# A hybrid decoder block on eight cores: SSM weight preparation on DVE, a fifth x buffer, u stores in POOL's queue, W_o casts later

## The reference, cut to what matters

```python
xn = rms_norm(x, g_pre_mix)
q, k, v, u = split(xn @ w_in)              # 1024, 256, 256, 1024 columns
attn = sliding_window_attention(rotary(q), rotary(k), v, sinks)   # window 128
y = s5_ssm(u)                              # 64 groups of 16 channels, 64 complex states each
z = gelu(y); ssm = z * sigmoid(z @ w_glu + b_glu)
mix = concat(rms_norm(attn), rms_norm(ssm)) @ w_o
h = x + rms_norm(mix)
out = h + rms_norm(swiglu(rms_norm(h)))    # gate, up: 2048 x 5632; down: 5632 x 2048
```

## Time and profile before

| | us |
|---|---|
| median of 3 runs (2626.15 to 2682.37) | 2632.01 |
| profiled execution, time | 2620.06 |
| profiled execution, span of the slowest core (core 3) | 2618.5 |
| span of the fastest core | 2595.2 |
| PE busy | 2445.9 (93%) |
| DVE, ACT, POOL busy | 1524.8, 848.9, 618.6 |

### The profile page before, as it was taken

One profiled execution on the slowest core, in us unless ns is written; L12 is line 12 of the kernel. 1 busy time (PEld: TensorE's weight loads), 2 busy tenths in 40 slices (PEclk: granted clock), 3 DMA queues, 4 the chain that ended last, 5 costly groups with the idle time before them and its releaser, 6 DMA issues.

```text
span 2618.5 us, 33812 instructions; the slowest of 8 cores (2595.2 to 2618.5 us)
## 1 busy us (share of the span) xinstructions
PE 2445.9 (93%) x12896; PEld 1203.6 (46%) x12896; DVE 1524.8 (58%) x2354; ACT 848.9 (32%) x1654; POOL 618.6 (24%) x708
## 2 busy tenths in 40 slices
PE   3797888987998989999999999999999999999998
PEld 2443656843444434444444444444444444444443
DVE  7735673668687687777777400016877877710003
ACT  7633443366565433223222100003222223200002
POOL 3334576854343200101010111100010101111112
PEclk9898888998999999999999999999999999999999
DMA  8499568466797977666766966649999876775557
GB/s 217 135 147 124 94 97 142 75 159 157 181 205 206 184 147 132 89 89 83 94 81 90 191 106 110 105 68 162 178 177 179 135 93 81 96 116 79 74 106 239
DMA packets 484893, 341.82 MB, mean 131 GB/s; under 512 B 182016, under 2 KB 448640, under 8 KB 475776
## 3 DMA queue, kind: packets, MB, share of 16 engines
q0 software_dynamic: 257744, 168.90, 47.4%
q1 hardware_dynamic: 226992, 170.77, 25.5%
HBM read 406.65 MB, written 63.96 MB: 180 GB/s over the span
## 4 chain that ended last, share of the span: by engine, by line
PE 81%; DMA 7%; DVE 6%; issue 2%; POOL 2%; ACT 1%; SPq 1%; POOLq 0%; DVEq 0%; ACTq 0%
PE ps L433 81%; DMA ws.6_48<-w_in 1%; DVE M1.2_44 L433 1%; DMA A1T.68_110<-A1.44_86 1%; SPq L433 1%; DMA raw.148_190<-w_up 1%; DMA PT.126_168<-Pb.123_165 1%; DMA uring.89_131<-uscr 0%; DVE ast.27_69 L433 0%; DMA A1T.66_108<-A1.44_86 0%; DVE hn.142_184 L433 0%; DMA raw.146_188<-w_gate 0%; DVE TT.49_91 L433 0%; DVE TT.50_92 L433 0%; DVE Rb.102_144 L433 0%
## 5 line engine op out<-in xcount | busy, mean ns | idle before, releaser
L433 DVE TENSOR_TENSOR hf.234_276<-ps,gpo.189_231 128x512 f32<-128x512 f32 x16 | 11.1, 691 | 243.4 <-ACT junk.144_186 L433 233.7
L433 ACT ACTIVATE junk.144_186<-ps 128x512 bf16<-128x512 f32 x48 | 28.6, 597 | 296.3 <-PE ps L433 291.1
L433 PE MATMUL ps<-hnT.143_185,wsm.151_193 128*128 128x512 bf16 x528 | 121.1, 379 | 0.4 <-DVE ev.171_213 L433 0.4
L433 PE MATMUL ps<-hnT.143_185,wsm.150_192 128*128 128x512 bf16 x528 | 121.3, 379 | 0.0
L433 PE MATMUL ps<-hnT.143_185,wsm.153_195 128*128 128x512 bf16 x528 | 121.1, 379 | 0.0
L433 PE MATMUL ps<-hnT.143_185,wsm.152_194 128*128 128x512 bf16 x528 | 121.1, 379 | 0.0
L433 ACT ACTIVATE ps<-ps 128x512 f32<-128x512 f32 x32 | 18.6, 582 | 294.8 <-DVE ev.175_217 L433 138.5
L433 DVE TENSOR_TENSOR wsm.153_195<-raw.149_191 128x1024 bf16<-128x1024 bf16 x110 | 68.6, 684 | 61.7 <-DMA raw.149_191<-w_gate 59.5
L433 POOL DMA_DIRECT2D raw.146_188<-w_gate x22 | 25.2, 1144 | 266.3 <-PE ps L433 182.8
L433 POOL DMA_DIRECT2D raw.148_190<-w_up x22 | 25.2, 1145 | 255.9 <-PE ps L433 117.4
L433 POOL DMA_DIRECT2D raw.149_191<-w_gate x22 | 25.1, 1141 | 251.6 <-PE ps L433 132.2
(11 more groups left out here) (1349 smaller groups left out, 6263.8 us busy)
## 6 DMA issues: line engine op xcount, KB each, us to landing
raw.146_188<-w_gate POOLq DMA_DIRECT2D x22, 1024.0 KB, 9.4
raw.147_189<-w_up POOLq DMA_DIRECT2D x22, 1024.0 KB, 9.4
raw.149_191<-w_gate POOLq DMA_DIRECT2D x22, 1024.0 KB, 11.2
raw.148_190<-w_up POOLq DMA_DIRECT2D x22, 1024.0 KB, 12.3
woscr<-w_o POOLq DMA_DIRECT2D x16, 512.0 KB, 8.4
xr.137_179<-x SPq DMA_DIRECT2D x8, 1024.0 KB, 7.2
xr.138_180<-x SPq DMA_DIRECT2D x8, 1024.0 KB, 6.3
hscr<-xr.137_179 SPq DMA_DIRECT2D x8, 1024.0 KB, 4.1
```

What stands on the lines that cost most here:

```text
L433: inst = getattr(eng, m)(*a, **kw)
```

## The change

1. x tiles have five buffers, the fifth in space that the GLU uses later, taken in the order `XBUF`. The buffers in `ws[1]` hold tiles 3, 4, 8 and 9 only. The first w_in load is cut by columns, and tiles from 4 on wait for the first part alone. Only the first halves of even tiles are copied by ACT, the others by DVE.
2. The rope tables wait for the scaling of the last x tile.
3. For blocks 0 to 2 `prep` makes `CL` on DVE; blocks 1 and 2 wait for the scaling of tile 13.
4. u is stored through POOL's queue, each block as soon as its last group is copied; the second half of u runs over token blocks inside column blocks.
5. The sums of k and q are made on DVE.
6. Six W_o casts wait for pairs 14 to 29, ten for copies of the rope; the casts of w_glu wait for pairs 16 to 25.
7. Smaller ones: the last token block of `M1` is scaled at priority 590; the output projection scales before it squares, and squares into PSUM; attention tiles are spread over one tile more; the load of unit 2 waits for tile 14.

```diff
-        xt = [sb("xt", o_, [128, 2048], F32) for o_ in (SO, SO + 8 * KB, WSO + 16 * KB, WSO + 24 * KB)]
+        xt = [sb("xt", o_, [128, 2048], F32) for o_ in (SO, SO + 8 * KB, c1 + 2944, WSO + 16 * KB, WSO + 24 * KB)]
+        XBUF = (0, 1, 2, 3, 4, 0, 1, 2, 3, 4, 0, 1, 2, 0, 1, 2)
...
-        load_w(0, 1536, wk=("wu",))
+        for i in range(2):
+            P.dma(ws[0][:, :, 256 * i:256 * i + 256], w_in_v[:, :, 1536 + 256 * i:1792 + 256 * i], q="gpsimd", wk=[("wu", i)])
...
-                P.dma(b[:, :], x[tt * 128:(tt + 1) * 128, :], rk=[("wu", 0), ("wu", 1)] if tt > 3 else ())
+                P.dma(b[:, :], x[tt * 128:(tt + 1) * 128, :], rk=[("wu", 0)] if tt > 3 else ())
...
-                if h == 0 or tt % 2 == 0:
+                if h == 0 and tt % 2 == 0:
                     A.activation(out=dst, in_=src, func=AF.Copy)
...
-        V.tensor_copy(out=posf[:, :], in_=posi[:, :])
+        P._dep(V.tensor_copy(out=posf[:, :], in_=posi[:, :]), xsop[15], True)
...
+            if b in (1, 2):
+                P._dep(first, xsop[13], True)
+            E = V if b < 3 else G
...
-            G.tensor_tensor(out=o(c, 9), in0=bc(Cf, 0, 9), in1=lk(0, 8, 9), op=ALU.mult)
+            E.tensor_tensor(out=o(c, 9), in0=bc(Cf, 0, 9), in1=lk(0, 8, 9), op=ALU.mult)
...
-            for tb in range(4):
-                for blk in range(4):
+            for n in range(16):
+                tb, blk = (n // 4, n % 4) if h == 0 else (n % 4, n // 4)
...
+                if n >= 12 if h == 0 else n % 4 == 3:
+                    c0 = (4 * h + blk) * 128
+                    P.dma(uscr[:, c0:c0 + 128, :].rearrange("j p c -> p j c"), ust[:, 3 - blk, :, :], q="gpsimd", wk=[("u", 4 * h + blk)])
...
-                G.tensor_tensor(out=qb, in0=rA[:, :], in1=rB[:, :], op=ALU.add)
+                V.tensor_tensor(out=qb, in0=rA[:, :], in1=rB[:, :], op=ALU.add)
...
-                E_ = G if i0 < 4 else V
+                E_ = V
...
+                if tb == 3:
+                    P.prio = 590.0
...
-                A.activation(out=junk[cb % 2][:, :], in_=ps[:, cb % 2, :], func=AF.Square, scale=1.0 / math.sqrt(D),
+                V.tensor_tensor(out=Ab[:, cs], in0=ps[:, cb % 2, :], in1=gpm[:, cs], op=ALU.mult)
+                A.activation(out=ps[:, cb % 2, :], in_=ps[:, cb % 2, :], func=AF.Square, scale=1.0 / math.sqrt(D),
                              accum_out=ss[:, cb:cb + 1])
-                V.tensor_tensor(out=Ab[:, cs], in0=ps[:, cb % 2, :], in1=gpm[:, cs], op=ALU.mult)
...
-                  rk=[("hn", 15)] if blk == 0 and u == 2 else (), lat=12.0 if blk == 0 and u < 2 else 0.0)
+                  rk=[("hn", 14)] if blk == 0 and u == 2 else (), lat=12.0 if blk == 0 and u < 2 else 0.0)
...
-            if q % 4 == 1:
-                cast_wo(4 + q // 8, q // 4 % 2, P.ops[-1])
-            if q % 4 == 3:
-                P.prio = 20.0
-                cast_wo(q // 8, q // 4 % 2, usteps[16 + q // 2])
+            if q in (14, 17, 20, 23, 26, 29):
+                cast_wo((14, 17, 20, 23, 26, 29).index(q), last)
-            if q % 8 == 4:
-                i = q // 8
-                P.dma(glscr[:, i, :], w_glu_v[:, 4 + i, :], q="gpsimd", after=(P.ops[-1],), wk=[("gl", i)])
+            if q in (16, 19, 22, 25):
+                i = (16, 19, 22, 25).index(q)
+                P.dma(glscr[:, i, :], w_glu_v[:, 4 + i, :], q="gpsimd", after=(last,), wk=[("gl", i)])
...
+        for n, i in enumerate((10, 18, 22, 26, 30, 34, 38, 42, 46, 50)):
+            P.prio = 62.0
+            cast_wo(6 + n, psteps[i])
...
-            for at in range(min(NT, LOOK + (NT - LOOK) * tt // (NT - 3)), min(NT, LOOK + (NT - LOOK) * (tt + 1) // (NT - 3))):
+            for at in range(min(NT, LOOK + (NT - LOOK) * tt // (NT - 2)), min(NT, LOOK + (NT - LOOK) * (tt + 1) // (NT - 2))):
```

More of the change, by code:

```diff
@@ L604, in frac @@
             V.tensor_tensor(out=dst, in0=src, in1=tmp, op=ALU.subtract)
+        xsop = []
         def xnorm(tt):
-            b, s = xt[tt % 4], xs[tt % 2]
+            b, s = xt[XBUF[tt]], xs[tt % 2]
             if tt > 0:
-                P.dma(b[:, :], x[tt * 128:(tt + 1) * 128, :], rk=[("wu", 0), ("wu", 1)] if tt > 3 else ())
+                P.dma(b[:, :], x[tt * 128:(tt + 1) * 128, :], rk=[("wu", 0)] if tt > 3 else ())
             ms, r = col(), col()
@@ L613, in xnorm @@
             rstd(r, ms)
-            V.scalar_tensor_tensor(out=s[:, :], in0=b[:, :], scalar=r, in1=gbc[:, :], op0=ALU.mult, op1=ALU.mult)
+            xsop.append(V.scalar_tensor_tensor(out=s[:, :], in0=b[:, :], scalar=r, in1=gbc[:, :], op0=ALU.mult, op1=ALU.mult))
             for h in range(2):
@@ L737, in prep @@
             CL, A1, A1T, kt = CLs[b % 3], A1s[b % 2], A1Ts[b % 3], KTs[b % 3]
-            V.tensor_tensor(out=o(a, 8), in0=bc(Bb, 0, 8), in1=lk(0, 0, 8), op=ALU.mult)
+            first = V.tensor_tensor(out=o(a, 8), in0=bc(Bb, 0, 8), in1=lk(0, 0, 8), op=ALU.mult)
+            if b in (1, 2):
+                P._dep(first, xsop[13], True)
+            E = V if b < 3 else G
             V.tensor_tensor(out=o(b_, 8), in0=bc(Bb, 1, 8), in1=lk(1, 0, 8), op=ALU.mult)
@@ L744, in prep @@
             P.dma(A1T[:, :, :], A1[:, :], transpose=True)
-            G.tensor_tensor(out=o(c, 9), in0=bc(Cf, 0, 9), in1=lk(0, 8, 9), op=ALU.mult)
[L746 to L750, removed]
+            E.tensor_tensor(out=o(c, 9), in0=bc(Cf, 0, 9), in1=lk(0, 8, 9), op=ALU.mult)
+            E.tensor_tensor(out=o(d, 9), in0=bc(Cf, 1, 9), in1=lk(1, 8, 9), op=ALU.mult)
+            E.tensor_tensor(out=oC(0), in0=o(c, 9), in1=o(d, 9), op=ALU.add)
+            E.tensor_tensor(out=o(c, 9), in0=bc(Cf, 1, 9), in1=lk(0, 8, 9), op=ALU.mult)
+            E.tensor_tensor(out=o(d, 9), in0=bc(Cf, 0, 9), in1=lk(1, 8, 9), op=ALU.mult)
+            E.tensor_tensor(out=oC(1), in0=o(c, 9), in1=o(d, 9), op=ALU.subtract)
             for par in range(2):
@@ L771, in bank3 @@
             return bk
-        usteps = []
         def proj_u(h):
             sl = ws[h % 2]
-            for tb in range(4):
-                for blk in range(4):
+            for n in range(16):
+                tb, blk = (n // 4, n % 4) if h == 0 else (n % 4, n // 4)
+                if True:
                     bk = bank3()
@@ L783, in proj_u @@
                                      rhs=xnT[:, c, tb * 512:(tb + 1) * 512], start=(c == 0), stop=(c == 15))
[L784 to L788, removed]
+                    A.activation(out=ust[:, 3 - blk, :, tb * 64:(tb + 1) * 64],
+                                 in_=ps[:, bk, :].rearrange("p (c j) -> p j c", j=8), func=AF.Copy)
+                if n >= 12 if h == 0 else n % 4 == 3:
+                    c0 = (4 * h + blk) * 128
+                    P.dma(uscr[:, c0:c0 + 128, :].rearrange("j p c -> p j c"), ust[:, 3 - blk, :, :], q="gpsimd", wk=[("u", 4 * h + blk)])
         RK = WSO + 16 * KB
@@ L809, in load_h @@
             return w
+        psteps = []
         def rope(bk, tt, n):
             rr, rA, rB = rbuf[n % 2]
-            A.activation(out=rr[:, :], in_=ps[:, bk, 0:256], func=AF.Copy)
+            psteps.append(A.activation(out=rr[:, :], in_=ps[:, bk, 0:256], func=AF.Copy))
             V.tensor_tensor(out=rA[:, :], in0=rr[:, :], in1=cap(cosT, tt * 32, [[512, 128], [0, 8], [1, 32]]), op=ALU.mult)
@@ L1046, in build_nc, with cast_wo @@
         woscr = dscr("woscr", [8, 128, 2, 2048], BF16)
-        def cast_wo(k, i, op):
-            P.dma(woscr[k, :, i, :], w_o_v[:, 2 * k + i, :], q="gpsimd", after=(op,), wk=[("wo", k, i)])
+        def cast_wo(n, op):
+            P.dma(woscr[n // 2, :, n % 2, :], w_o_v[:, n, :], q="gpsimd", after=(op,), wk=[("wo", n // 2, n % 2)])
         def load_wo(k):
@@ L1287, in build_nc @@
             P.prio = 60.0 + q
-            if q % 4 == 1:
-                cast_wo(4 + q // 8, q // 4 % 2, P.ops[-1])
-            if q % 4 == 3:
-                P.prio = 20.0
-                cast_wo(q // 8, q // 4 % 2, usteps[16 + q // 2])
-            if q % 8 == 4:
-                i = q // 8
-                P.dma(glscr[:, i, :], w_glu_v[:, 4 + i, :], q="gpsimd", after=(P.ops[-1],), wk=[("gl", i)])
+            last = P.ops[-1]
+            if q in (14, 17, 20, 23, 26, 29):
[3 more added lines that the diff above has]
+                P.dma(glscr[:, i, :], w_glu_v[:, 4 + i, :], q="gpsimd", after=(last,), wk=[("gl", i)])
             if q % 4 == 3 and q < 20:
```

## The result

The changed kernel took 2659.71 us (median of 6, 2652.69 to 2747.14) against 2629.08 for the kernel before (6 runs beside it, 2623.73 to 2682.37): a ratio of 1.0109, 95% interval 1.0076 to 1.0142. So it is about 1% slower, inside the 2% that the prediction took for no change. The forecast was 2570, with a range of 2538 to 2612.

What follows compares the result with a forecast made beforehand. The prediction took TensorE's idle and low-clock time before 957 us as the bound; terms -33 + 2 - 22 + 3 - 6 - 6 = -62 gave 2558 for the profiled execution and 2570 for the median, range 2538 to 2612.

Steps and rivals of the forecast that it cites:

- Front, -33 to 114: 0 to 147 us: earlier x tiles and cheaper prep end the first half of u at 114, saving 33 (19 to 41).
- Transposes, -22: Stall at 225 to 267: moving W_o casts away ends late A1 transposes, saving 22 (8 to 28).
- u stores, +2: Before the first u tile: eight u stores in POOL's queue land later, costing 2 (0 to 10).
- the hold-up of +5.5: u stores: if DVE copies of 0.69 held up each of eight POOL stores, their cost would be +5.5, not +2.
- K and q, +3 (-10 to +22): 300 to 545 us: ten casts arrive and 48 sums move from POOL to DVE, costing 3 net.
- The rival with casts at 4.4: K and q stretch: ten moved casts cost 4.4 each, 44 instead of 3, giving 2611; chance 0.07.
- the slower rival: 300 to 480 us: late transposes in the rope's four-buffer ring stop DVE, ten costing 137, giving 2704; chance 0.05.
- the prediction's own sign of being wrong: K and q stretch: DVE waiting on kT or qT transposes would show the forecast wrong; no size given.
- Output projection, 0 (-4 to +4): Output projection and attention spread: same instructions in another order, so no cost or gain, ends -4 and +4.
- Third gate load, -6: After transpose 15 (945.45): the load starts some 6.6 us sooner, after tile 14, saving 6 (3 to 7).
- GLU, -6: GLU and first W_o groups, from 630: eight M1 scalings drop to a later place, saving 6 (0 to 9).

Runs made afterwards that it cites:

- the front: The kernel before with only points 1 to 3 of the change: ratio 0.9903 to the kernel before, median 2605 us.
- the front and the casts: The kernel before with points 1 to 3 and 6 (W_o casts later), sums on POOL, u stores on SP: ratio 1.0074, median 2650 us.
- the experiment for that: The kernel before with points 1 to 3, the second w_in load waiting for the last x tile's scaling: ratio 0.9905, median 2606 us.

## Why the prediction was wrong, step by step

**Front, -33 to 114: right, a little large.** Core 4's first group starts at 39.41 (40 said), the fifth x tile is asked for at 34.03 (31.9), DVE's 512-wide products of 49 to 110 take 684 ns on core 6. The half ends at 122 without the 0.81 stretch, so -27, inside the bounds. One thing was left out: only the first two blocks need the first weight part, and for the next two TensorE waited until 51.60:

```profile
39.41 9.38 PE L433 MATMUL ps<-xnT.1_43,ws.6_48 128*128 128x512 bf16 x32 [0.99 <-DVE xnT.1_43 L433]
...
51.60 7.07 PE L433 MATMUL ps<-xnT.1_43,ws.6_48 128*128 128x512 bf16 x32 [1.92 <-DMA ws.6_48<-w_in]
```

**Transposes, -22: the cause right, the size too large.** From the front's lead of 27 the lead grows to 44 at the last A1T product: -17, of which 9 is work put off (see K and q), so -8, the upper bound. On core 6 four of the five A1 transposes of 120 to 330 landed in 2.8 to 5.0 and one in 12.3, which nothing waited for over 2.2. The casts were the cause: moving them alone, on the front, brings the same product 18 sooner.

**u stores, +2: right only because the casts had left.** The A1T column is the same with point 4 (332) and without (332, the front and the casts). The eight issues took about 0.9 us each on core 6, so the hold-up of +5.5 that the prediction set beside it did not show. Behind the eleven old casts the same stores cost some 12, a price that no term had.

**K and q, +3 (-10 to +22): this step failed.** The stretch grew by 25, for two reasons. Here it is for all of TensorE's products and for those with `wh.9_51`, one of the three projection tiles, first before (core 3), then in the changed kernel (core 6); the tile's lines have no DVE and ACT:

```profile
384.00:536.00 152.00, 138.49 (x1230) 115.90 (x1227) 83.23 (x152) 58.78 (x110) 112.65 (x192) 0.94 0.68 107
384.00:536.00 152.00, 30.59 (x256) 24.67 (x256) 1.19 (x1) 0.94 0.68 107
...
329.00:505.00 176.00, 151.50 (x1311) 125.44 (x1312) 102.64 (x202) 59.69 (x114) 100.94 (x174) 0.92 0.86 122
329.00:505.00 176.00, 42.97 (x336) 33.74 (x336) 2.39 (x2) 0.92 0.86 122
```

Eighty products, five groups of 16 at some 1.8 us, had run ahead of the last A1T product and now run behind it: 9 us put off, not lost. The other 16 are the casts, since without them, and with the same five groups, the stretch is 160. The reason given, that TensorE has rope-independent groups to run, did not hold: it is idle for 24.5 of 176 instead of 13.5 of 152. So +16 stood inside the bounds, but the value took the low row although a row of before gave 4.4 a cast and another the 8.89 wait; ten casts measured 1.6 each here and 2.2 on the front alone. The rival with casts at 4.4 named the place rightly and the price too high; the slower rival named the queue (on core 6 DVE waited 12.2 for one kT transpose, the prediction's own sign of being wrong), but the sums on DVE are innocent, since POOL waits in DVE's place with the same loss.

**Output projection, 0 (-4 to +4): this step failed.** It measured +16 in the changed kernel and +20 by itself. "Same instructions, other order" overlooked that the last reader frees the PSUM bank, and that ACT, with 1 to 2 us operations ahead of its squares, is a worse last reader than DVE.

**Third gate load, -6: failed.** The load was issued sooner after the last W_o product, and yet TensorE waited 7.20 instead of 4.48. Core 4:

```profile
971.71 1.14 POOL L433 DMA_DIRECT2D raw.147_189<-w_gate  x1 [25.34 <-PE ps L433]
...
980.12 3.09 DVE L433 TENSOR_TENSOR wsm.152_194<-raw.148_190 128x1024 bf16<-128x1024 bf16 x5
982.35 0.14 PEld L433 LDWEIGHTS ps<-hnT.144_186,raw.147_189 128*128 128x128 bf16 x2 [7.66 <-issue]
982.38 3.57 PE L433 MATMUL ps<-hnT.144_186,raw.147_189 128*128 128x512 bf16 x8 [7.20 <-DMA raw.147_189<-w_gate]
...
985.75 2.11 PE L433 MATMUL ps<-xe.157_199,wsm.152_194 128*128 128x512 bf16 x8
```

In the new plan unit 2's product (`raw.147`) stands ahead of unit 1's (`wsm.152`), which used to run while it travelled. From the last W_o product to the last gate or up product it takes 3 longer than before; how much of that is this edit is not shown, since with point 7 undone it takes no less. **GLU, -6:** +3; on the front alone the later M1, with the spread, moved nothing.

The sum without the clock: -27 - 8 + 0 + 16 + 3 + 16 + 3 = 3, against 4 in the spans (2612 and 2608).

**The clock was not in the sum.** In the profiled execution the 0.81 stretch adds 31 on the cores that have it. Over the executions low pairs of the changed kernel were 9 of 20 and ended 24 later (2645 against 2621). In the kernel before a low pair ends 13 to 16 later, and fewer are low: on three chips 6 of 56, 25 of 80 and 24 of 84 pairs of the kernel before, against 24 of 64, 70 of 104 and 58 of 124 of the kernels with the new front. As the slowest of eight cores sets the time, and each of the five executions of the changed kernel has a low pair, all of them pay. Taking the casts out of 205 to 260 made the pay larger, 31 instead of 14 on the front: TensorE's idle time from 75 to 245, 24 with the front alone (core 4) and 14 with the casts moved (core 0, neither with the stretch), had probably hidden part of it.

What stays open is why the stretch comes more often with the new front, and why it takes pairs; the experiment for that fell on a chip that showed none.

## What to carry to other kernels

Traffic that is moved away from one stall must be priced at the place where it arrives, by a row from a like queue: ten casts beside the rope's transposes took back more than their leaving gave. A stage that is read from its last product must be read with a count of the work that moved across that mark: 9 of the 44 that the changed kernel led by were groups not yet run. An edit that changes only who reads a PSUM bank last is no free edit: look at what stands ahead of the new last reader in its engine. And where a static order is drawn up anew from modelled times, any edit can move work out of the gap that it was filling.

## What the hardware showed that was not expected

The granted clock has a value between its two levels: 0.81, in the changed kernel on both cores of a pair within 0.2 us of each other (each from its own start). In the profiled executions it began mostly at 74 to 81. In the changed kernel the clock had risen to 1.00 some 4 to 6 us before, and the stretch was over 161 to 164 after its start, on core 4 with TensorE full to the end of it. The Trainium skill, page "TensorE: Matmul & The Clock Gate", section "Seeing it yourself", has a limiter that takes a whole die to 13/16 once a third core runs dense products, and holds it while the load lasts. The value agrees (13/16 is 0.8125). The rest differs in these runs: cores 4 and 5 had it and 6 and 7 of the same die had not, and in 985 to 1790 core 4 was full for 805 us at 1.00. The measurement decides.
